# A two-block transformer kernel on one core: the first modulation in pairs of chunks with reordered loads, and the weight halves placed 48 bytes past a multiple of 64

## The reference, cut to what matters

```python
def first_block(x, c, ...):
    c_act = jax.nn.silu(c)
    for l in range(2):
        mod = c_act @ w_ada[l] + b_ada[l]                    # 1024 -> 6 * 1024
        sh1, sc1, gt1, sh2, sc2, gt2 = jnp.split(mod, 6)
        h = rms_norm(x, norm_mix[l]) * (1.0 + sc1) + sh1
        proj = h @ w_in[l]                                   # 1024 -> 7440
        ...                                                  # delta rule, window attention
        x = x + gt1 * (merged @ w_o[l])
        h = rms_norm(x, norm_ffn[l]) * (1.0 + sc2) + sh2
        ...                                                  # gated FFN, 2816 wide
        x = x + gt2 * (... @ w_down[l])
def second_block(x, ...):                                    # per layer: FFN, hybrid mixer, FFN
    ...
```

## Time and profile before

| | us |
|---|---|
| runs shown | 2249.02, 2247.62, 2246.27; median 2247.62 |
| profiled execution | 2247.91 |
| its span, first to last instruction | 2246.1 |
| TensorE busy in the span | 2167.6 (97%) |
| VectorE / ScalarE / GpSimd busy | 1507.6 / 1072.3 / 581.1 |
| HBM traffic over the span | 170 GB/s mean |

### The profile page before, as it was taken

One profiled execution on the slowest core, in us unless ns is written; L12 is line 12 of the kernel. 1 busy time (PEld: TensorE's weight loads), 2 busy tenths in 40 slices (PEclk: granted clock), 3 DMA queues, 4 the chain that ended last, 5 costly groups with the idle time before them and its releaser, 6 DMA issues.

```text
span 2246.1 us, 39818 instructions
## 1 busy us (share of the span) xinstructions
PE 2167.6 (97%) x17241; PEld 2077.4 (92%) x17241; DVE 1507.6 (67%) x1856; ACT 1072.3 (48%) x1420; POOL 581.1 (26%) x280
## 2 busy tenths in 40 slices
PE   7999999999999999999999999989999999999999
PEld 7988899999989888989999999879999999879999
DVE  6867776677678776667666556876556556786555
ACT  2566573443456647443445335554445334555333
POOL 0863314899248250476000000100000000100000
PEclk7999999999999999999999999999999999999999
DMA  9752335677657315566555555325555555424553
GB/s 292 230 183 77 114 129 189 225 244 244 208 169 226 95 39 168 169 206 207 182 181 176 182 183 168 113 94 188 188 183 174 185 181 179 132 94 151 180 182 126
DMA packets 332856, 383.93 MB, mean 171 GB/s; under 512 B 12551, under 2 KB 315402, under 8 KB 332554
## 3 DMA queue, kind: packets, MB, share of 16 engines
q1 hardware_dynamic: 332234, 381.23, 52.7%
q10 hardware_dynamic: 448, 0.16, 0.0%
HBM read 380.32 MB, written 1.05 MB: 170 GB/s over the span
## 4 chain that ended last, share of the span: by engine, by line
PE 78%; DVE 13%; ACT 7%; issue 2%; DMA 0%; SPq 0%; ACTq 0%; DVEq 0%
PE bank L736 16%; PE bank L737 16%; PE bank L738 16%; DVE weights_low L1387 5%; PE bank L974 5%; PE bank L976 5%; PE bank L975 5%; ACT weights_high L2086 3%; DVE arena L1487 1%; PE bank L752 1%; PE bank L1020 1%; PE bank L875 1%; PE bank L1011 1%; PE bank L1171 1%; PE bank L776 1%
## 5 line engine op out<-in xcount | busy, mean ns | idle before, releaser
L1387 DVE TENSOR_TENSOR weights_low<-ring,weights_high 128x2048 fp32r<-128x2048 f32 x302 | 751.5, 2488 | 442.0 <-ACT weights_high L2086 441.6
L736 PE MATMUL bank<-h_high,weights_high 128*128 128x256 f32 x3296 | 944.3, 287 | 22.8 <-DVE weights_low L1387 13.5
L737 PE MATMUL bank<-h_low,weights_high 128*128 128x256 f32 x3296 | 927.7, 281 | 0.0
L738 PE MATMUL bank<-h_high,weights_low 128*128 128x256 f32 x3296 | 927.3, 281 | 0.0
L2086 ACT ACTIVATE weights_high<-ring 128x2048 fp32r<-128x2048 f32 x302 | 578.1, 1914 | 703.4 <-PE bank L738 549.1
L736 PEld LDWEIGHTS bank<-h_high,weights_high 128*128 128x128 f32 x3296 | 622.5, 189 | 41.8 <-DVE weights_low L1387 22.5
L737 PEld LDWEIGHTS bank<-h_low,weights_high 128*128 128x128 f32 x3296 | 623.3, 189 | 3.5 <-issue 3.3
L738 PEld LDWEIGHTS bank<-h_high,weights_low 128*128 128x128 f32 x3296 | 623.1, 189 | 0.0
L974 PE MATMUL bank<-hidden_high,weights_high 128*128 128x256 f32 x1056 | 299.1, 283 | 1.3 <-DVE hidden_low L1625 0.8
L975 PE MATMUL bank<-hidden_low,weights_high 128*128 128x256 f32 x1056 | 298.4, 283 | 0.0
L976 PE MATMUL bank<-hidden_high,weights_low 128*128 128x256 f32 x1056 | 298.4, 283 | 0.0
(11 more groups left out here) (423 smaller groups left out, 2851.9 us busy)
## 6 DMA issues: line engine op xcount, KB each, us to landing
ring<-in_w_in SPq DMA_DIRECT2D x80, 1024.0 KB, 5.3
ring<-in_w_up SPq DMA_DIRECT2D x44, 1024.0 KB, 5.2
ring<-in_ffn_w_gate SPq DMA_DIRECT2D x44, 1024.0 KB, 5.3
ring<-in_ffn_w_up SPq DMA_DIRECT2D x44, 1024.0 KB, 5.4
ring<-in_ffn_w_down SPq DMA_DIRECT2D x44, 1024.0 KB, 4.9
side<-in_w_ada SPq DMA_DIRECT2D x42, 1024.0 KB, 7.7
ring<-in_w_down SPq DMA_DIRECT2D x22, 1024.0 KB, 4.9
ring<-in_w_dn_out SPq DMA_DIRECT2D x8, 1024.0 KB, 5.2
```

Source lines behind the costliest of these rows:

```text
L736: mm(o[:, m, :], a_, high[:, t, :], start=(t == 0), stop=False)
L737: mm(o[:, m, :], a_, low[:, t, :], start=False, stop=False)
L738: last = mm(o[:, m, :], b_, high[:, t, :], start=False, stop=(t == KT - 1))
L1387: v.tensor_tensor(low, wide(q), high.bitcast(F32), ALU.subtract).then_inc(chunk_split, 1)
```

## The change

It has two parts.

**Opening.** The eight chunks are taken in four pairs, each of a shift chunk i and a scale chunk 4 + i. Shift chunks go to PE with the operands exchanged: `weigh_row` has a column of c stationary and 256 columns of weights moving, 8 matmuls a chunk into one row of bank B[3]; ACT copies that row (`row_out`, to `modrow`), and `columns` turns it into two columns with two small matmuls and sums the two scale columns of `acc` with two more. Scale chunks go to DVE (`modulate`), one fewer than before. As soon as a pair is there, DVE makes the two columns of bias and scale (`modulate_pair`), ACT applies them to two tiles of x and rounds (`head_rounded`, four instructions), DVE makes the low halves (`low_tiles`) and PE multiplies these two tiles with `s1` (`head_tiles`). x is multiplied by the norm factor in one DVE instruction beforehand. The loads are in the order chunk 0, chunk 4, `s1`, chunks 1, 5, 2, 6, then `qkv` 0, chunks 3 and 7. The vectors of the first layer land and are turned ahead of the rest. DVE and ACT split `qkv` 0 inside the opening and `qkv` 1 before the keys' small work. POOL starts behind the split of `qkv` 1.

**Placement.** The four halves are views at element 12 (48 bytes) of stores that are 2192 elements apart, so each starts 48 bytes past a multiple of 64. `arena` grows by 64 elements (256 bytes); what lies behind it moves by that and keeps its remainder.

```diff
-ADA_V = (4, 6, 7, 0)
-ADA_RING = (5, 1)
+ADA_V = (1, 5, 2, 6)
+ADA_RING = (0, 4)
...
-        WH = [rounded(f"weights_high{i}", 14336 + 2 * SLOT * i, KT, T) for i in range(2)]
-        WL = [rounded(f"weights_low{i}", 14336 + SLOT + 2 * SLOT * i, KT, T) for i in range(2)]
+        half_stores = [rounded(n, 14336 + (SLOT + 16) * i, SLOT + 16) for i, n in enumerate(half_names)]
+        shifts = (12, 12, 12, 12)
+        half = lambda i, n: half_stores[i][:, shifts[i]:shifts[i] + KT * n].rearrange("p (t n) -> p t n", t=KT)
+        WH, WL = ([half(2 * i + low, T) for i in range(2)] for low in range(2))
...
+            def weigh_row(i):
+                ...
+                row = B[3][0:1, (i % 2) * T:(i % 2) * T + T]
+                for t in range(KT):
+                    last = mm(row, ccol[:, t:t + 1], w[:, t, :], start=(t == 0), stop=(t == KT - 1))
...
+            def head_tiles(*tiles):
+                ...
+                for t in tiles:
+                    pe.wait_ge(norm_ready, t + 1)
...
-            weigh_ring(5)
             pe.wait_ge(x_done, 4)
+            weigh_row(0)
             for u in range(4):
                 sum_pair(0, u)
...
+            columns(0)
+            weigh_row(1)
+            columns(1)
+            head_tiles(0, 1)
+            weigh_row(2)
+            columns(2)
+            head_tiles(2, 3)
...
+            weigh_row(3)
+            columns(3)
+            head_tiles(4, 5)
+            head_tiles(6, 7)
...
             modulate(0)
+            dve.wait_ge(vectors_turned, 1)
+            then(v.tensor_copy(vcol[:, 0, 0:V_ROWS[0]], B[0][:, 0:V_ROWS[0]]))
+            dve.wait_ge(norm_factor, 1)
+            v.tensor_tensor(tmp[:, :, :], x[:, :, :], over(rinv[:, :], KT), ALU.mult).then_inc(x_normed, 1)
+            modulate_pair(0)
             modulate(1)
+            split(1)
+            low_tiles(0)
+            modulate_pair(1)
             modulate(2)
+            low_tiles(1)
...
```

More of the change, by code:

```diff
@@ L1028, in reduce_start @@
[L1028 to L1034 removed]
+            def weigh_row(i):
+                if i == 0:
+                    q = Q["ada", 0, ADA_RING[0]]
+                    pe.wait_ge(w_landed[q % NS], landed[q])
+                    w = slot(q)[:, 0:2 * D].rearrange("p (t n) -> p t n", t=KT)
+                elif i < 3:
+                    pe.wait_ge(start_landed[2 * i - 2], 16)
+                    w = start_at[2 * i - 2]
+                else:
+                    pe.wait_ge(side_landed[0], 16)
+                    w = side[0][:, :].rearrange("p (t n) -> p t n", t=KT)
+                if i >= 2:
+                    pe.wait_ge(row_copied, i - 1)
+                row = B[3][0:1, (i % 2) * T:(i % 2) * T + T]
+                for t in range(KT):
+                    last = mm(row, ccol[:, t:t + 1], w[:, t, :], start=(t == 0), stop=(t == KT - 1))
+                last.then_inc(row_weighed, 1)
@@ new lines, in columns @@
+            def columns(i):
+                shift, scale = (L[R["adr", 0, g] % 2] for g in range(2))
+                pe.wait_ge(row_copied, i + 1)
+                for m in range(2):
+                    at = STEP * (2 * i + m)
+                    last = mm(shift[:, at:at + 1], modrow[0:1, i % 2, m * P:(m + 1) * P], ones[0:1, 0:1], start=True, stop=True)
+                last.then_inc(shift_summed, 1)
+                pe.wait_ge(chunk_modulated, i + 1)
+                for m in range(2):
+                    at = STEP * (2 * i + m)
+                    last = mm(scale[:, at:at + 1], acc[:, 1, (2 * i + m) * P:(2 * i + m + 1) * P], ones[:, 0:1], start=True, stop=True)
+                last.then_inc(scale_summed, 1)
@@ new lines, in head_tiles @@
+            def head_tiles(*tiles):
+                n = SI["s1", 0, 0]
+                wh, wl = halves(n)
+                pe.wait_ge(chunk_split, n + 1)
+                for t in tiles:
+                    pe.wait_ge(norm_ready, t + 1)
+                    for tt in range(2):
+                        a_, b_ = h_high[:, t, tt * P:(tt + 1) * P], h_low[:, t, tt * P:(tt + 1) * P]
+                        to = B[4 + tt][:, 0:WIDE]
+                        mm(to, a_, wh[:, t, :], start=(t == 0), stop=False)
+                        mm(to, a_, wl[:, t, :], start=False, stop=False)
+                        last = mm(to, b_, wh[:, t, :], start=False, stop=(t == KT - 1))
+                if tiles[-1] == KT - 1:
+                    last.then_inc(chunk_multiplied, 1)
@@ L1407, in modulate, with modulate_pair, low_tiles @@
                         ins.then_inc(chunk_modulated, 1)
+            def modulate_pair(i):
+                shift, scale = (L[R["adr", 0, g] % 2][:, STEP * 2 * i:STEP * (2 * i + 2):STEP] for g in range(2))
+                two = lambda at: slice(at + 2 * i, at + 2 * i + 2)
+                dve.wait_ge(shift_summed, i + 1)
+                ins = v.tensor_tensor(modc[:, two(0)], shift, vcol[:, 0, two(0)], ALU.add)
+                if i < 3:
+                    then(ins)
+                else:
+                    ins.then_inc(mod_ready, 1)
+                dve.wait_ge(scale_summed, i + 1)
+                ins = v.tensor_tensor(modc[:, two(KT)], scale, vcol[:, 0, two(KT)], ALU.add)
+                if i < 3:
+                    then(ins)
+                else:
+                    ins.then_inc(mod_ready, 1)
+                    dve.wait_ge(mod_ready, 2)
+                v.scalar_tensor_tensor(out=scol[:, two(0)], in0=modc[:, two(KT)], scalar=1.0, in1=vcol[:, 0, two(VA["norm_mix"])],
+                                       op0=ALU.add, op1=ALU.mult).then_inc(pair_modulated, 1)
+            def low_tiles(i):
+                for t in (2 * i, 2 * i + 1):
+                    dve.wait_ge(h_rounded, t + 1)
+                    v.tensor_tensor(h_low[:, t, :], tmp[:, t, :], h_high[:, t, :].bitcast(F32), ALU.subtract).then_inc(norm_ready, 1)
             def modulation(l, g):
                 n, va = GROUPS.index((l, g)), VT[0, l]
-                dve.wait_ge(mod_summed, n + 1)
+                dve.wait_ge(mod_summed, n - 1)
                 cols = modc[:, KT * g:KT * g + KT]
@@ L2268, in _ @@
                 a_(sm(3), sm(3), ACT.Ln, bias=col(COL_ONE), scale=1.0).then_inc(d_e, 1)
-                split(SI["qkv", l, 0] + 2)
+                if l == 0:
+                    act.wait_ge(start_v, 2)
+                    a_(nea[:, :], heads[:, R_ALOG:R_ALOG + 16], ACT.Exp).then_inc(start_a, 1)
                 act.wait_ge(keys_turned, l + 1)
```

180 lines of the change are left out of this document (104 added, 76 removed).

## The result

The changed kernel takes 2234.28 us, median of 6 runs (2232.28 to 2236.26), for 2247.57 before: a ratio of 0.9943, 95% interval 0.9933 to 0.9953. That is -13.3 us. The forecast was 2233.0, with 2206 to 2255 as its range. Its profiled execution took 2234.28 too, its span 2232.5.

A forecast was written before the change was run, and what follows sets the result against it. The prediction took TensorE, busy 97% of the span, as the bound: a number of matmuls times their distance, plus an opening. 2247.9 - 9.6 (placement) - 5.3 (opening) = 2233.0 us, range 2206 to 2255.

The forecast's parts named there:

- the removed wait: TensorE's wait of 2.14 us ahead of the second `qkv` chunk, forecast to go as its low half is done earlier.
- rival D: Opening: clock stays at 0.50 from 22, last two `weigh_row` 3.4 us more each, +5 for -5.3; 2243.3; chance 0.15.
- that of `h`: Placement term of the 9888 matmuls with `h` moving: no change taken, bounds 14.8 us gained to 16.8 us lost.
- The four rows: Traced matmul distances before: `h` 118.3, `attended` 120.0, hidden 119.6, weights moving 116.8 ns; the only evidence for placement.
- the middle of two rows: 117.5 ns, between 116.8 and 118.3, taken for hidden, `attended` and the other streams: -9.6 us together.
- The stated bounds: Limits on matmul distances after placement: `h` 116.8 to 120.0 ns, hidden and the rest 116.8 to 118.3.
- C: Placement: operands starting in the same 32-byte half of 64 bytes cost; `h` at 120.0, +16.8 us; 2253.8; chance 0.20.
- B: Placement gives nothing, matmul distances belonging to partner banks or instruction mix; only the opening's -5.3, 2242.6 us; chance 0.17.

The follow-up runs named there:

- e11: The changed kernel with ACT and DVE splitting `qkv` 1 behind the keys' small work again, as in the kernel before: 2237.16 us.
- e7: The changed kernel with all four weight halves at 64 modulo 256 bytes and the old spacing of 8704 bytes: 2215.52 us.
- e10: The changed kernel with all four weight halves at 0 modulo 256 bytes and the old spacing: 2250.2 us.
- e3: The changed kernel with the first pair of weight halves 16 bytes past a multiple of 64 and the second pair 32: 2233.83 us.
- e1: The kernel before with only the four weight halves moved to the change's placement, old opening kept: 2238.56 us, ratio 0.9963.
- e9: e7 with `h`, the arena and the weight halves all 64 bytes further on, differences between operands kept: 2213.55 us.
- e12: e7 with rows 2 and 3 weighed ahead of the preceding pair's tiles, and the last pair ahead of the split of `qkv` 0: 2212.17 us.
- e5: The changed kernel with all four weight halves at 144 modulo 256 bytes and the old spacing: 2247.3 us.
- e2: The changed kernel with the weight halves back at multiples of 64, their stores still 8768 bytes apart: 2237.92 us.

## Why the prediction was right, and where it was not

**The opening: right, step by step.** Forecast: third pair out at 40.9, `weigh_row(3)` done at 47.8, last pair at 49.8, `s1` done at 53.6, `qkv` 1 at 59.9. Measured: 41.7, 47.7, 49.7, 53.5, 59.5. The two microseconds of the removed wait were the split of `qkv` 1 (e11). -5.3 forecast, -5.7 measured; as the other traces of this opening start `qkv` 1 at 58.5 to 61.2, so close a hit is partly luck. One thing in it was too pessimistic for this trace: the first `weigh_row` ran at the higher clock (3.61 us for 16 records; in e7, where the clock rose only at 15.8, it took 5.42), so TensorE wasn't late there; the landing of chunk 1 and the `modulate` of chunk 5 were. The clock then fell at 27.3, behind a stretch (24.0 to 27.3) in which TensorE was busy for 1.29 of 3.30 us, and was back at 37.5:

```profile
26.00:30.00 4.00, 1.02 (x4) 0.66 1.11 345
30.00:34.50 4.50, 2.90 (x12) 0.50 1.10 347
34.50:40.00 5.50, 5.12 (x17) 0.73 1.10 348
```

`weigh_row(2)` took 5.04 us for 3.61, 1.4 us, where rival D had 3.4 for each of the last two, and the last one ran at the higher clock. So D didn't happen, but a piece of it did.

**Placement: right in size, wrong in its rule.** Hidden 117.6 and the rest 117.5 for a forecast of 117.5; `h` 118.5 for 118.3, as the mean of two pairs of halves of which neither was at 118.3. In us: 3168 x (119.7 - 117.6) = 6.7 and 1152 x (119.9 - 117.5) = 2.8 won, 9888 x 0.2 = 2.0 lost, where -9.6 and 0 had been forecast, and the 288 with weights moving lost 1.4 ns each, 0.4. Together -7.1, and with the opening -12.8 for -13.6 between the two profiled executions. The term that was mis-sized is that of `h`: 0.2 ns over 9888. The remaining 0.8 us was not traced.

The step that failed without showing in the number is the one ahead of it: that one operand at 0 and the other not, modulo 64, makes the pace. The four rows it was read from are true, but places modulo 64 were one label out of many for them. Three placements with the same label gave `h` 119.9, 117.0 and 118.3 (e10, e7, before); "no change for `h`" and the middle of two rows for the others came out by what these places happen to have: the number was luck. The forecast had named this as a way to be wrong, a rule for 32 against 48 that none of its four rows shows. The stated bounds of 116.8 and 120.0 for `h` held for this change and for every placement tried as a mean over a trace; those for hidden, 116.8 to 118.3, did not: its means went from 114.3 (e7) to 119.2 (e3). The outcome that C feared, `h` near 120, exists at another placement (119.9 in e10).

**The rivals.** B (nothing by placement) falls with e1: 0.9963, interval below 1. With it falls the 16-byte line as the whole answer. The Trainium skill (SBUF — State Buffer, Specifications) states cachelines of 16 bytes with a penalty for each crossing to a new one; by that alone, starts at multiples of 16 are alike. The traces disagree: such starts range from 113.4 to 123 ns. The Trainium skill (SBUF — State Buffer, Who interferes with whom) states that TensorE reads its moving operand and its weights through two independent ports; by that, each operand's place would count by itself. Between the kernel before and e7 only the weights' place differs in these streams, so all of them would move alike. The traces disagree with that too: `h` went from 118.3 to 117.0, `attended`, in the same loop, from 119.9 to 117.8, and hidden from 119.7 to 114.3. And e9, with all operands moved together, left `h` where it was. C falls: it wanted `h` at 120.0, and 48 against 32 ran at 119.0 to 119.3 with one pair and 117.6 to 117.9 with the other. D, see above.

**What stays open.** What sets the pace. The runs show that it depends on the operands' places, over more than 64 bytes, and for `h` on the relative ones as far as one shift tells; that one placement can have several paces for the same matmuls (113.4 and 117.8; 117.7, 118.4 and 123); and that such a pace holds from the first dozen matmuls of a chunk to its end. A table by the difference modulo 256 was tried and fell. What picks the pace at a chunk's start was not found. All of it is read from one trace a kernel.

## What to carry over

Where one engine is 97% busy with a few thousand equal instructions, read the distance between their starts, chunk by chunk, and not the rounded mean of the records alone: 1 ns over the `h` matmuls was 10 us here, and a mean hides that a stream has several paces. Where operands lie in SBUF is then a parameter to be measured, not derived: move all the weights through a few places and take the trace, since a rule drawn from four rows gave the right number once, and the better table drawn from six traces missed by 23 to 38 us in its first three uses. And of a shorter chain ahead of TensorE, look at how much arrives there and at the granted clock just behind it: in e12 2.3 us on DVE became 1.2 on TensorE, and the lower clock took 2.3.

## What was not expected of the hardware

- The same fp32r matmul of 128x128 by 128x256 came at distances from 113.4 to 123 ns as a chunk's mean, with nothing but the places of its operands in SBUF changed, and within one placement from chunk to chunk: 2250.2 to 2213.6 us for a kernel whose instructions are the same (e10, e9), 1.6%.
- Two paces for one placement, 5.33 or 5.54 us a chunk (e9), 5.53 or 5.77 (e5). The runs of e5 spread over 16 us, where the changed kernel's six lie within 4; that the paces make the spread is not shown, since only one of its runs has a trace.
- Sixty-four bytes more between the stores of the halves, with every half at a multiple of 64, took 2.3 ns off the hidden stream and added 0.5 to that of `h` (e2).
